# Loading v in four transfers of 4 KB per partition, and 384 dense columns with 136 gathered slots, in a hybrid decoder step

## What is computed

```python
q = rms_norm(einsum('td,dq->tq', hb, w_query).reshape(PEER_BLOCK, PEER_HEADS, PEER_DKEY), qnorm_g)
# scores against two sets of 128 subkeys, top 16 of each half, then the top 16 of the 256 sums, per head
e = i1[ci // 16] * 128 + i2[ci % 16]          # expert ids: 8 heads x 16 per token
g = softmax(sc)
a = gelu(einsum('td,ted->te', hb, u[e]))
y = einsum('te,ted->td', g * a, v[e])         # v is 16384 x 1024, float32
```

## Time and profile before

| | before |
|---|---|
| median of three runs | 1784.61 us (1782.64 to 1786.2) |
| the profiled execution | 1801.27 us, its span 1799.5 us |
| TensorE busy | 1757.9 us (98%) |
| VectorE, ScalarE, GpSimd busy | 1226.7, 566.1, 513.2 us |
| moved by DMA | 399.21 MB, 222 GB/s on average |
| gathers of activations and of rows | 144 and 144 |
| dense products of the down half (L2154) | 3072 matmuls |

### The profile page before, as it was taken

How to read it: one execution, slowest core, us unless ns; L and a number is a source line. 1 busy time by engine, 2 the same in 40 slices (tenths; PEclk the granted TensorE clock), 3 DMA queues, 4 the chain that set the end, 5 groups by cost and what they waited for, 6 DMA issues and landing times.

```text
span 1799.5 us, 31088 instructions
## 1 busy us (share of the span) xinstructions
PE 1757.9 (98%) x12693; PEld 1309.9 (73%) x12693; DVE 1226.7 (68%) x2566; ACT 566.1 (31%) x942; POOL 513.2 (29%) x563
## 2 busy tenths in 40 slices
PE   8999998999999999999999999999979999999999
PEld 7743446788888887898888888888746666666666
DVE  7559877769989948787455555544247777676764
ACT  1012235402333233454344444434212222222220
POOL 0000201021656712000000000000278777777760
PEclk9999999999999999999999999999989999999999
DMA  4432723021123333766888888966489999999991
GB/s 170 109 109 71 278 95 142 1 94 74 48 95 119 143 143 113 274 250 268 286 311 289 298 301 298 297 242 222 161 322 361 349 366 350 352 356 349 358 350 60
DMA packets 137230, 399.21 MB, mean 222 GB/s; under 512 B 13824, under 2 KB 86768, under 8 KB 125312
## 3 DMA queue, kind: packets, MB, share of 16 engines
q1 hardware_dynamic: 108816, 315.81, 47.4%
q0 software_dynamic: 28272, 81.42, 13.1%
HBM read 320.72 MB, written 76.45 MB: 221 GB/s over the span
## 4 chain that ended last, share of the span: by engine, by line
PE 85%; DVE 12%; issue 2%; ACT 1%; DMA 0%; DVEq 0%; ACTq 0%
PE psum L2106 34%; PE psum L2154 28%; PE psum L1807 19%; PE psum L2127 2%; DVE u_lo L1543 1%; PE psum L1822 1%; PE psum L1813 1%; PE psum L1936 0%; DVE rest L1470 0%; DVE sdm L1347 0%; PE psum L1959 0%; PE psum L1859 0%; DVE ixs L1487 0%; DVE CI L1516 0%; DVE CI L1508 0%
## 5 line engine op out<-in xcount | busy, mean ns | idle before, releaser
L2154 PE MATMUL psum<-w_hl,v_hi 128*128 128x376 bf16 x2048 | 492.8, 324 | 3.7 <-issue 3.7
L2106 PE MATMUL psum<-h_hi,u_hi 128*128 128x260 bf16 x2048 | 396.1, 275 | 2.8 <-DVE u_lo L1543 2.1
L2106 PE MATMUL psum<-h_lo,u_hi 128*128 128x260 bf16 x2048 | 395.9, 275 | 0.0
L2106 PE MATMUL psum<-h_hi,u_lo 128*128 128x260 bf16 x2048 | 395.9, 275 | 0.0
L777 POOL DMA_INDIRECT t_dots<-d_acts,t_lists x144 | 173.0, 1201 | 629.1 <-issue 629.1
L2154 PE MATMUL psum<-w_hl,v_lo 128*128 128x376 bf16 x1024 | 331.6, 324 | 5.7 <-issue 5.7
L2154 PEld LDWEIGHTS psum<-w_hl,v_hi 128*128 128x128 bf16 x2048 | 201.1, 98 | 133.1 <-issue 9.9
L1715 DVE TENSOR_TENSOR v_lo<-v_raw,v_hi 128x1024 bf16<-128x1024 f32 x128 | 148.2, 1220 | 134.5 <-issue 107.8
L1543 DVE TENSOR_TENSOR u_lo<-u_raw,u_hi 128x1024 bf16<-128x1024 f32 x128 | 154.3, 1221 | 121.2 <-ACT u_hi L985 121.1
L1014 ACT ACTIVATE v_hi<-v_raw 128x1024 bf16<-128x1024 f32 x128 | 124.8, 1046 | 355.6 <-PE psum L2154 321.5
L2106 PEld LDWEIGHTS psum<-h_hi,u_hi 128*128 128x128 bf16 x2048 | 197.8, 97 | 34.1 <-DVE u_lo L1543 2.4
(11 more groups left out here) (399 smaller groups left out, 1822.2 us busy)
## 6 DMA issues: line engine op xcount, KB each, us to landing
u_raw<-in_uT SPq DMA_DIRECT2D x32, 2048.0 KB, 9.5
v_raw<-in_v SPq DMA_DIRECT2D x32, 2048.0 KB
wr<-in_w SPq DMA_DIRECT2D x13, 2048.0 KB, 7.7
d_gate<-stage SPq DMA_DIRECT2D x12, 2048.0 KB, 7.2
w_hl<-d_w SPq DMA_DIRECT2D x32, 768.0 KB
g_up<-d_gate SPq DMA_DIRECT2D x18, 768.0 KB, 9.2
d_w<-w_up SPq DMA_DIRECT2D x18, 768.0 KB, 9.5
d_act<-act_f SPq DMA_DIRECT2D x14, 768.0 KB, 3.9
```

The lines of the kernel that those rows point to most:

```text
L2106: mm = pe.matmul(upair[n % 2][:, f, 0:HALF], w[g % 2][:, k, c * P:(c + 1) * P], hs[:, k, halves[f]], start=(k == 0 and x == 0), stop=(k == ...
L2154: mm = pe.matmul(ybank[m][:, 0:DENSE], w[g % 2][:, c, m * P:(m + 1) * P], w_hl[g % WRING][:, z, c, 0:DENSE], start=(g == 0 and c == 0 and ...
```

## The change

DENSE becomes 384: the 8 EXTRA tokens join the dense part, so that each matmul of L2154 has 384 columns in place of 376, and the gates have 96 quads in place of 94. Their 8 slots, lists, transfers, `x_acc` and the selecting matmul go; TSLOTS is 136, and the pacing formulas follow it. `load_v` issues four transfers of 512 KB, 4 KB per partition each; `v_high` still waits for all four.

```diff
-GATED = SEQ - P
-EXTRA = 8
-DENSE = GATED - EXTRA
-NBLK = GATED // TB
+DENSE = SEQ - P
+NBLK = DENSE // TB
-XSLOTS = SSLOTS + EXTRA * H * TOPK // P
-TSLOTS = XSLOTS + H * TOPK
+TSLOTS = SSLOTS + H * TOPK
-KEPT = EXTRA + P + DB
+KEPT = P + DB
...
             def load_v(j):
                 if j >= 2:
                     sp.wait_ge(vlo_done, 4 * (j - 1))
-                sp.dma_start(v_raw[j % 2][:, :, :].rearrange("p c d -> p (c d)"), I["v"][j]).then_inc(v_in[j % 2], 16)
+                for c in range(GC):
+                    sp.dma_start(v_raw[j % 2][:, c, :], I["v"][j][:, c * D:(c + 1) * D]).then_inc(v_in[j % 2], 16)
...
-            for half in range(HALVES):
-                for h in range(H):
-                    at = EXTRA * (H * half + h)
-                    pool.dma_start(t_lists[at:at + EXTRA, :, SSLOTS:XSLOTS],
-                                   x_lists[P - EXTRA:P, :, h * TOPK + half * (XSLOTS - SSLOTS):][:, :, 0:XSLOTS - SSLOTS]
-                                   ).then_inc(s_moved, 16)
...
-            pool.wait_ge(s_moved, MOVED)
+            pool.wait_ge(s_moved, 32)
...
             def v_high(g):
-                act.wait_ge(v_in[g % 2], (g // 2 + 1) * 16)
+                act.wait_ge(v_in[g % 2], (g // 2 + 1) * 16 * GC)
...
-            tail = slice(P - COLT, P)
-            first, second = idx[tail, NPT - 2, 0, :], idx[tail, NPT - 2, 1, :]
-            sdo(v.tensor_copy(x_gate[tail, :], gt[tail, NPT - 2, :]))
-            sdo(ts(t_who[tail, :], t_who[tail, :], -float(P), None, ALU.add))
...
-            sdo(v.tensor_reduce(xsel[:, :], ident.rearrange("p (h t) -> p t h", t=EXTRA), AX.X, ALU.add))
...
-                if i == 1:
-                    v.wait_ge(s_moved, MOVED)
...
-                            mm = pe.matmul(ybank[m][:, 0:DENSE], w[g % 2][:, c, m * P:(m + 1) * P], w_hl[g % WRING][:, z, c, 0:DENSE],
+                            mm = pe.matmul(ybank[m][:, 0:DENSE], w[g % 2][:, c, m * P:(m + 1) * P], w_hl[g % WRING][:, z, c, :],
...
-                        product(ybank[m][:, DENSE:GATED], [(x_acc[:, m * P:(m + 1) * P], xsel[:, :])])
-                        turn(ybank[m][:, GATED:SEQ], t_acc[:, m * P:(m + 1) * P], P).then_inc(y_made, 1)
+                        turn(ybank[m][:, DENSE:SEQ], t_acc[:, m * P:(m + 1) * P], P).then_inc(y_made, 1)
```

## The result

On the same chip the changed kernel takes 1788.35 us (median of 20 runs, 1786.47 to 1791.39) and the kernel before 1784.88 us (20 runs, 1782.36 to 1787.83): ratio 1.0022, 95% interval 1.0016 to 1.0028. That is +3.9 us in the ratio's terms (+3.5 between the medians); the prediction said 1788.4 us. The profiled execution of after is 1788.27 us with a span of 1786.4 us. It is 13.0 us shorter than the profiled execution of before, although the kernel is slower. So what follows first takes apart which of the trace's differences belong to the change. Two timed executions of the experiments lie far off (7661.82 us of the kernel before beside e9, 2874.3 us of e8), and no ratio counts them.

The account below looks back on a forecast made before the run. TensorE, busy 98% of the span, was taken to bound the kernel. The terms 10.1 + 0.9 - 1.0 - 3.3 - 2.95 = +3.8 us on 1784.6 gave 1788.4 us, range 1779 to 1796 us.

Parts of the forecast that it names:

- Columns, +10.1: Down half: eight more columns on 3072 dense matmuls, all on TensorE's path, cost 10.1 us.
- The rival that they are not paid: Down half: TensorE in truth waits for something, giving 1778 us; chance 0.18 together with a half-way stall case.
- Two quads, +0.9: Gates: two more quads, 16 matmuls at 0.0575 us each on the path, cost 0.9 us.
- The end, -1.0: End of the 8 output tiles: the selecting matmul pair goes, 0.12 us each, -1.0 us; VectorE's slots are no limit.
- The lists, -3.3: First gates: VectorE comes 3.44 us earlier without twelve list operations; TensorE's 4.28 us of waits become 1.0, -3.3 us.
- The clock, -2.95: Behind the first gates' wait: the granted clock stays up instead of falling to 0.50, -2.95 us, 0 as other end.
- the row at 336 us: Sign that the clock stays up at the first gates: a wait of 1.58 us at 336 us left it at 1.00.
- the clock falls all the same: Rival at the first gates: the 2.95 us stay, so +6.7 us, 1791.3 us; chance 0.18.
- v in four transfers, 0 out of 0 to +6: Down half's loads of v: smaller pieces cost +0.57 us a group but stay hidden: 0, bounds 0 to +6 us.
- transfers become the pace: Rival in the down half: v comes late by 0.2 us or more per group, 1794 us and more; chance 0.06.
- The stall: Early down half, 1317 to 1336 us: 15.7 us lost in the profiled execution, likely (three in four) not in timed runs.
- small pieces end the stall: Rival in the down half's first 45 us: timed runs stall too, quarter-size packets end it, 1772.7 us; chance 0.12.

Follow-up runs that it names:

- e9: The changed kernel unchanged, run again beside the kernel before on a chip of the slower kind: 1800.65 us, ratio 1.0005.
- e8: The changed kernel with v in sixteen transfers of 1 KB per partition: 1788.69 us, ratio 1.0021 to the kernel before.
- e2: The kernel before with the down half's dense products 384 columns wide in place of 376: 1807.12 us, ratio 1.0050.
- e7: The changed kernel with the twelve list operations put back, results unused: 1793.06 us, ratio 1.0049 to the kernel before.
- e6: The changed kernel with its list operations moved ahead of the copies of the tables: 1787.17 us, ratio 1.0012 to the kernel before.
- e1: The kernel before with v in four transfers of 4 KB per partition, nothing else: 1796.44 us, ratio 0.9986.
- e3: The kernel before with all list operations of the slots moved ahead of the copies of the tables: 1791.94 us, ratio 0.9967.
- e10: The kernel before with its list operations ahead of the copies of the tables and v in four transfers: 1789.09 us, ratio 0.9948.
- e4: The changed kernel with v in one transfer of 16 KB per partition: 1799.3 us, ratio 1.0000 to the kernel before.
- e5: The changed kernel unchanged, run again beside the kernel before on another group's chip: 1787.92 us, ratio 1.0020.
- e11: The kernel before with its list operations ahead of the copies of the tables, the same kernel as e3, run again: 1776.34 us, ratio 0.9960.
- e12: The kernel before with GpSimd's gathered rows of v held until TensorE has done the first group: 1783.92 us, ratio 1.0001.

## Why the prediction came out right, and where its reason was not

*Columns, +10.1.* Measured +10.2 (159.2 to 162.5 ns on 3072 matmuls), paid in full; e2 alone gave +9.0 (6.7 to 11.3 by its interval). The rival that they are not paid falls.

*Two quads, +0.9.* The balance has 0.9 us between the first gates and the down half.

*The end, -1.0.* With the columns it makes the down half's +9.0: right within 0.2 us, and VectorE's slots were no limit.

*The lists, -3.3.* Waits of 4.28 us became 1.02. e7 puts them back, and e6's profile is without the last one.

*The clock, -2.95.* This was called the least sure term, taken by the row at 336 us. It held: granted 1.00 behind a wait of 1.02 us, and 0.50 again in e7 behind waits of 2.97 and 1.32 us. The rival "the clock falls all the same" (+6.7) falls.

*What was not in the sum.* Wait and clock make 6.25 us by the sum and 5.8 to 6.1 by the profiles; between the profiles of before and after the gain is 7.7 up to the gates. The rest is from 613 to 616 us, where before does 14 matmuls fewer. After, then before:

```profile
613.00:616.00 3.00, 3.00 (x29) 2.59 (x28) 3.00 (x18) 1.45 (x2) 1.15 (x4) 1.00 1.06 334
```

```profile
613.00:616.00 3.00, 3.00 (x15) 2.09 (x14) 3.00 (x17) 1.00 (x2) 1.27 (x2) 0.50 1.08 347
```

Both have a wait of TensorE for `u_low` just ahead (2.56 us in after, 2.11 in before), in code that the change does not touch; the clock fell behind the shorter one. In the twelve other profiles the clock is 1.00 in this stretch, with 27 to 30 matmuls, in those of kernels built on before too; so it was one execution's chance, and I count it to neither kernel.

*v in four transfers, 0 out of 0 to +6.* Right: every conversion of v is still released by TensorE (349.5 of 349.5 us), and e8 shows that even 1 KB pieces stay hidden. In after the parts of v land 7.0 us after their issue and the products 12.2 (medians), well inside the lead of 24.8 us. The trace's packet times from 1340 to 1760 us bear out the price of 0.57 us a group that the prediction took from the gathered rows: a row of v takes one packet of 16 KB and 650 ns on average in before, four packets of 181 ns in after, 74 ns more, and a group has eight rows for each of 16 DMA engines: 0.59 us, all of it hidden. The rival in which transfers become the pace falls. On the chips with the stall, e1 gave -2.5 us (-4.3 to -0.7) and the pair e3 and e10, on two chips, -3.4; but after with four transfers (e9, 1.0005) is no better there than with one (e4, 1.0000). Whether small pieces shorten that stall a little is open.

*The stall.* The prediction said, three chances in four, that the stall is not in the timed runs, and put the sum on top of 1784.61 us. For the timed runs of this measurement that was true, and it gave the right number. But the prediction took the stall for something that a profiled execution has and timed runs lack, and named no reason. The runs show that it goes with the chip: where the profiles show it, the timed runs are longer by about as much, and seven profiled executions (after, e5 to e8, e11, e12) are without it. The same kernel, by the medians of its sets of runs:

| kernel | without the stall | with it | more |
|---|---|---|---|
| before | 1783.4 to 1784.9 | 1799.2, 1799.6 | 14.3 to 16.2 |
| after (e5 and the result, e9) | 1787.9, 1788.4 | 1800.7 | 12.3 to 12.7 |
| lists first (e11, e3) | 1776.3 | 1791.9 | 15.6 |

The profiled 1801.27 us of before and its timed 1784.61 then look like two such kinds of chip side by side; no run shows this, since the chips of those executions are not on record. What was luck is that the measurement fell on a chip without the stall. On one with it the prediction would have been 1803 us, by its sentence that the same sum holds if the stall stays. That did not hold: there the change costs nothing that can be measured (e9, four transfers: +0.9 us, -1.1 to +2.9; e4, one transfer: 0, -2.0 to +1.8). The stall is not a constant that drops out of the difference. By the lengths of the down half in the profiles it takes 15.8 us in before and e3, 11.9 and 11.1 in e1 and e10, 10.0 in e4 and 14.1 in e9, one execution each. The rival "small pieces end the stall" falls with e9: the stall was there with 4 KB pieces. The Trainium skill's rule that a DMA engine goes round its queues by packets ("DMA: Bandwidth & Descriptors", queues, rings and completion order), on which that rival leaned, is not contradicted by this; what falls is that TensorE's stall hangs on it.

What makes the stall on those chips is **not settled**. Known: it begins in stretches where the DMA engines are nearly full, no engine is named as waited for, its place moves (1300 to 1336 us, or 1480 to 1510), and the page of every such execution lacks the landings of v and of the products, which the others have (e8 those of the products alone). Instructions that come late, or transfers of which the trace lost the record, would both look so. From the timeline of before, four rows in a row, and the page's line on one DMA queue:

```profile
1325.28 0.32 PE L2154 MATMUL psum<-w_hl,v_lo 128*128 128x376 bf16 x1 [0.77 <-issue]
1326.00 0.50 PE L2154 MATMUL psum<-w_hl,v_hi 128*128 128x376 bf16 x1 [0.40 <-issue]
1326.70 0.47 PE L2154 MATMUL psum<-w_hl,v_hi 128*128 128x376 bf16 x1 [0.21 <-issue]
1328.12 0.47 PE L2154 MATMUL psum<-w_hl,v_lo 128*128 128x376 bf16 x1 [0.94 <-issue]
```

```profile
q8 instruction: 100, 1.64, 0.4%
```

The starts are 0.72, 0.70 and 1.42 us apart. Through the stalls of before, e2, e4 and e9 TensorE runs small groups, one to five matmuls, and one group starts about 0.7, 1.4 or 2.1 us behind the other. The 100 packets of that queue have 16 KB each, and the trace times them. They keep step with TensorE's count of matmuls, stall or not: in e9 such packets start behind 9677, 9809 and 9925 matmuls, in e5 behind 9677, 9805 and 9921. In before one starts at 1335.5 us, where the stall ends; but in e9, at 1316.8 us, one starts in the midst of it, and TensorE goes on in dribs. So these packets, taken as a whole, do not explain the stall, and what gives the step of 0.7 us stays open. e12, which was to thin out the load at that place, ran where there was nothing to see.

## What to carry to other kernels

Where one engine is busy 98% of the span, price a change by what that engine executes: 8 columns on 3072 matmuls came out at 10.2 us for 10.1, while 25 us less on GpSimd, and all of VectorE's 10 us but the 3.44 that TensorE waited for, came out at nothing. A few short operations ahead of a wait can cost twice, once as the wait and once as the clock behind it (twelve operations of 3.44 us: 5.1 us timed, 6.0 in the profile), so look first whether they can be moved to where their engine idles: e11 had that gain without paying for the columns. And before a gap between a profiled execution and the timed runs goes into a sum, run the same kernel on a second chip.

## What the hardware showed that I had not expected

On two of the experiments' four chips the kernels that ran on both kinds took 12 to 16 us more, by a stall of TensorE that begins at full DMA load and in which it restarts in steps of about 0.7 us; the changed kernel took 1787.92 and 1788.35 us in two sets of runs and 1800.65 us in the third. A granted clock of 0.50 followed a wait of 2.11 us in one execution and not one of 2.56 us in another, at the same place of the program; at the first gates it followed the two long waits in five profiles of five. v in pieces of 1 KB raised the DMA engines' share from 0.90 to 0.96 at unchanged GB/s and time.
